# Turning the finished y with DRAM scratch transfers and 32x32 block transposes on VectorE instead of TensorE transposes

## What is computed

```python
h = rms_norm(x, norm_g)
proj = h @ w_in                              # 4096 x ~14000
y_a = sigmoid(ao) * rms_norm(mlstm(...)) * silu(az)      # 1024 columns
y_b = sparse_attention(...) * silu(bz)                   # 2048 columns
y_c = rms_norm(gated_delta(...)) * silu(cz)              # 1024 columns
y = concatenate([y_a, y_b, y_c], axis=-1)    # 256 x 4096
return x + y @ w_out                         # w_out 4096 x 4096
```

## Time and profile before

| what | us |
|---|---|
| median of 3 runs | 1605.11 (1604.88 to 1605.93) |
| the profiled execution, its own time | 1605.32 |
| its span in the trace | 1603.6 |
| PE busy | 1593.8 (99%) |
| DVE busy | 933.5 (58%) |
| ACT busy | 769.3 (48%) |
| POOL busy | 31.3 (2%) |

### The profile page before, as it was taken

How to read it: one execution, slowest core, us unless ns; L and a number is a source line. 1 busy time by engine, 2 the same in 40 slices (tenths; PEclk the granted TensorE clock), 3 DMA queues, 4 the chain that set the end, 5 groups by cost and what they waited for, 6 DMA issues and landing times.

```text
span 1603.6 us, 19082 instructions
## 1 busy us (share of the span) xinstructions
PE 1593.8 (99%) x7456; PEld 1318.2 (82%) x7456; DVE 933.5 (58%) x1410; ACT 769.3 (48%) x1044; POOL 31.3 (2%) x60
## 2 busy tenths in 40 slices
PE   8999999999999999999999999999999999999999
PEld 6888888888888888888778888888888888888887
DVE  5655555557667445574488565564446666665454
ACT  6644444487443334454545455454445434444332
POOL 1000000000011000000000000000001000000000
PEclk9999999999999999999999999999999999999999
DMA  8656666756567554556555555556665655556674
GB/s 290 185 174 206 186 195 184 189 160 185 156 197 210 158 155 145 159 171 192 163 158 178 175 173 163 163 174 206 187 190 187 235 175 171 182 173 195 190 243 158
DMA packets 164006, 294.15 MB, mean 183 GB/s; under 512 B 22458, under 2 KB 27212, under 8 KB 163916
## 3 DMA queue, kind: packets, MB, share of 16 engines
q1 hardware_dynamic: 161084, 284.02, 58.5%
q0 software_dynamic: 2832, 8.92, 1.7%
HBM read 288.17 MB, written 4.72 MB: 183 GB/s over the span
## 4 chain that ended last, share of the span: by engine, by line
PE 98%; DVE 1%; ACT 0%; DMA 0%; issue 0%; SPq 0%
PE acc L584 30%; PE acc L586 30%; PE acc L585 30%; PE mix L557 3%; PE mix L683 2%; PE mix L805 1%; PE mix L665 0%; PE mix L786 0%; DVE w_lo L1248 0%; PE mix L641 0%; PE mix L824 0%; DMA w_raw<-in_w_in_dram 0%; ACT w_hi L917 0%; PE mix L783 0%; PE mix L768 0%
## 5 line engine op out<-in xcount | busy, mean ns | idle before, releaser
L1248 DVE TENSOR_TENSOR w_lo<-w_raw,w_hi 128x1024 fp32r<-128x1024 f32 (+1 forms) x536 | 646.1, 1217 | 468.5 <-ACT w_hi L917 466.2
L584 PE MATMUL acc<-w_hi,op_hi 128*128 128x512 f32 (+1 forms) x2048 | 815.5, 398 | 0.9 <-DVE w_lo L1248 0.9
L586 PE MATMUL acc<-w_hi,op_lo 128*128 128x512 f32 (+1 forms) x2048 | 800.4, 391 | 0.0
L585 PE MATMUL acc<-w_lo,op_hi 128*128 128x512 f32 (+1 forms) x2048 | 798.8, 390 | 0.0
L917 ACT ACTIVATE w_hi<-w_raw 128x1024 fp32r<-128x1024 f32 (+1 forms) x536 | 557.5, 1050 | 461.2 <-PE acc L586 452.6
L586 PEld LDWEIGHTS acc<-w_hi,op_lo 128*128 128x128 f32 x2048 | 385.0, 188 | 82.2
L584 PEld LDWEIGHTS acc<-w_hi,op_hi 128*128 128x128 f32 x2048 | 385.6, 188 | 79.7 <-DVE w_lo L1248 2.7
L585 PEld LDWEIGHTS acc<-w_lo,op_hi 128*128 128x128 f32 x2048 | 385.9, 188 | 75.5
L1380 DVE SCALAR_TENSOR_TENSOR cT<-mix,par,cT 128x255 f32<-128x255 f32 (+2 forms) x72 | 29.1, 474 | 18.2 <-ACT cT L1009 18.2
L1148 ACT ACTIVATE b_p<-b_s,st 128x128 f32<-128x128 f32 (+1 forms) x32 | 14.2, 446 | 49.1 <-DVE st L1585 49.1
L584 PE MATMUL acc<-w_hi,cq_hi 128*128 128x512 f32 x84 | 33.9, 403 | 0.0
(11 more groups left out here) (270 smaller groups left out, 764.2 us busy)
## 6 DMA issues: line engine op xcount, KB each, us to landing
w_raw<-in_w_in_dram SPq DMA_DIRECT2D x368, 512.0 KB, 4.0
w_raw<-in_w_out_dram SPq DMA_DIRECT2D x128, 512.0 KB, 3.8
w_raw<-in_w_in_dram SPq DMA_DIRECT2D x16, 384.0 KB, 3.4
w_raw<-in_a_wuq_dram SPq DMA_DIRECT2D x12, 512.0 KB, 3.8
xs<-in_x_dram SPq DMA_DIRECT2D x7, 512.0 KB, 6.7
w_raw<-in_a_wuqi_dram SPq DMA_DIRECT2D x6, 512.0 KB, 3.5
y<-in_x_dram POOLq DMA_DIRECT2D x6, 512.0 KB, 8.9
out_dram<-y POOLq DMA_DIRECT2D x5, 512.0 KB, 6.1
```

What stands on the lines that cost most here:

```text
L584: nc.tensor.matmul(o, hi[:, kt, tok], hv[:, i, :], start=(kt == blk["kts"][0]), stop=False)
L585: nc.tensor.matmul(o, hi[:, kt, tok], lv[:, i, :], start=False, stop=False)
L586: last_mm = nc.tensor.matmul(o, lo[:, kt, tok], hv[:, i, :], start=False, stop=(kt == blk["kts"][-1]))
L1248: vec.tensor_tensor(split_ap(w_lo, c), w_raw[:, c % RAW_BUFS, 0:n], split_ap(w_hi, c).bitcast(F32), ALU.subtract).then_inc(lo_ready, 1)
```

## The change

PE has no part in "yt" any more, and the piece uses no PSUM bank. In its place:

- POOL moves y through a DRAM scratch, in two parts: r = 1 (columns 1024 to 4095) after "bo" (3, 2) and c_y, r = 0 (columns 0 to 1023) after the last "ay". For each part it issues 8 stores from 32 partitions each, in runs of 32 fp32 numbers (128 B), waits for all 8, and issues 8 loads into 32 partitions each, in runs of 256 numbers (1 KB), back into the same columns of y. A store of r = 1 has 32 x 96 = 3072 runs, a load 32 x 12 = 384; for r = 0 these are 1024 and 128. After this every 32x32 block stands at its place, not yet turned inside.
- A new piece "yd" i on DVE transposes the 32x32 blocks of 128x512 numbers of y in place. "yd" 4 to 15 are in slots 367, 369, ... 389; each waits for all 8 loads of its part.
- "yt" i on ACT and DVE reads y in SBUF instead of the bank. ACT waits for "yd" i and for PE to be done with the slice of op_hi that it overwrites. "yt" 4 to 15 are now in slots 398 to 409; "yd" i and "yt" i for i = 0 to 3 together in slots 481, 483, 485 and 487.
- The reload of x comes behind the stores and loads of r = 1 on POOL; its six loads into y wait for 12 "yt" low parts. The stores and loads of r = 0 come behind the reload.

```diff
@@ plan()
-    weave(first + 4, [("yt", i) for i in range(4, 16)])
+    weave(end("aqk", 0) + 8, [("yd", i) for i in range(4, 16)], 2)
+    weave(first + 6, [("yt", i) for i in range(4, 16)])
...
-    at = weave(at + 1, [("yt", i) for i in range(4)], 2)
+    at = weave(at + 8, [[("yd", i), ("yt", i)] for i in range(4)], 2)
@@ layout
+        y_range = [(0, W_A // P), (W_A // P, KT)]
+        y_dram = [nc.dram_tensor(f"y_dram{r}", (32, z - a, 4, 4 * M, 32), F32) for r, (a, z) in enumerate(y_range)]
+
+        def y_columns(i):
+
+            r = 0 if 2 * i < W_A // P else 1
+            a, z = y_range[r]
+            n = (z - a) // M
+            k = 2 * i - a
+            return y[:, k // n, a * P + SEQ * (k % n):a * P + SEQ * (k % n) + 2 * SEQ]
@@ gpsimd
+            def y_blocks(r):
+
+                a, z = y_range[r]
+                n = (z - a) // M
+                for m in range(M):
+                    for i in range(4):
+                        pool.dma_start(y_dram[r][:, :, :, 4 * m + i, :].rearrange("a k j b -> a (k j) b"),
+                                       y[32 * i:32 * i + 32, m, a * P:z * P].rearrange("p (f b) -> p f b", b=32)
+                                       ).then_inc(y_kept[r], 16)
+                pool.wait_ge(y_kept[r], 16 * 4 * M)
+                for q in range(M):
+                    for j in range(4):
+                        pool.dma_start(y[32 * j:32 * j + 32, q, a * P:z * P].rearrange("p (k t) -> p k t", k=n),
+                                       y_dram[r][:, q * n:q * n + n, j].rearrange("a k i b -> a k (i b)")
+                                       ).then_inc(y_moved[r], 16)
+
             wait_read(pool, "bo", (HKV - 1, 2))
+            pool.wait_ge(c_y, len(UNITS))
+            y_blocks(1)
             for n in range(D // 512):
                 if 512 * n == W_A:
-                    for i in range(12, 16):
-                        wait_read(pool, "yt", i)
+                    pool.wait_ge(y_lo_ready, KT // 2 - 4)
                 pool.dma_start(out_acc(n), x_dram[:, :, 512 * n:512 * n + 512]).then_inc(x_again[n], 16)
+            pool.wait_ge(a_y, H_A)
+            y_blocks(0)
@@ tensor
-                        wait_read(pe, "yt", kt // 2)
+                        pe.wait_ge(y_lo_ready, (kt // 2 + 12) % 16 + 1)
...
-            def yt(i, use):
...
-                for j in range(2):
-                    for m in range(M):
-                        ins = turn(bank(use)[:, j * SEQ + m * P:j * SEQ + m * P + P],
-                                   y[:, m, (2 * i + j) * P:(2 * i + j) * P + P])
-                end_fill(ins, use)
@@ scalar, yt
-                wait_filled(act, use)
+                y_split[0] += 1
+                act.wait_ge(y_turned, y_split[0])
+                b_av = next(b for b, x_ in enumerate(blocks) if x_["kind"] == "av" and x_["arg"] == 1)
+                if i < KT // 2 - 1:
+                    act.wait_ge(split_used, last[b_av] - (KT // 2 - 1) + i + 1 - b_av)
+                else:
+                    act.wait_ge(acc_ready, b_av + 1)
...
-                    ins = func(op_hi[:, kt, :], bank(use)[:, j * SEQ:j * SEQ + SEQ], ACT.Copy,
+                    ins = func(op_hi[:, kt, :], y_columns(i)[:, j * SEQ:j * SEQ + SEQ], ACT.Copy,
@@ vector
+            def yd(i, use):
+                dve.wait_ge(y_moved[0 if i < 4 else 1], 16 * 4 * M)
+                vec.transpose(y_columns(i), y_columns(i)).then_inc(y_turned, 1)
+
             def yt(i, use):
...
-                    src, hi = bank(use)[:, j * SEQ:j * SEQ + SEQ], op_hi[:, kt, :].bitcast(F32)
+                    src, hi = y_columns(i)[:, j * SEQ:j * SEQ + SEQ], op_hi[:, kt, :].bitcast(F32)
...
-                done_bank(ins, use)
+                ins.then_inc(y_lo_ready, 1)
```

More of the change, by code:

```diff
@@ L83 @@
         "ck": 1, "cs": 1, "cr": 1, "co": 2, "bt": 1, "bkt": 2, "bit": 2, "bsc": 2, "bqt": 2, "bs": 1, "bp": 1,
-        "bo": 1, "at": 2, "ae": 2, "ap": 1, "yt": 1}
+        "bo": 1, "at": 2, "ae": 2, "ap": 1}
 def plan():
@@ L352, in hybrid_kernel @@
         y_hi_ready = sem("y_hi_ready")
+        y_kept = [sem(f"y_kept{r}") for r in range(2)]
+        y_moved = [sem(f"y_moved{r}") for r in range(2)]
+        y_turned = sem("y_turned")
+        y_lo_ready = sem("y_lo_ready")
         x_again = [sem(f"x_again{n}") for n in range(D // 512)]
@@ L864, in _ @@
                           cs=cs, cr=cr, co=co, bt=bt, bkt=bkt, bit=bit, bsc=bsc, bqt=bqt, bs=bs, bp=bp, bo=bo,
-                          at=at, ae=ae, ap=ap, yt=yt)
+                          at=at, ae=ae, ap=ap)
             def x_columns(i):
@@ L1174, in ap @@
                 ins.then_inc(a_ss, 1)
+            y_split = [0]
             def yt(i, use):
-                wait_filled(act, use)
+                y_split[0] += 1
[5 more added lines that the diff above has]
+                    act.wait_ge(acc_ready, b_av + 1)
                 for j in range(2):
@@ L1657, in _ @@
                           co=co, cy=cy, bn=bn, bt=bt, bkn=bkn, bqn=bqn, bsc=bsc, btk=btk, bts=bts, bs=bs, bo=bo, at=at, ae=ae, ap=ap, ay=ay,
-                          yt=yt)
+                          yd=yd, yt=yt)
             def x_lo(i):
```

## The result

The changed kernel takes 1621.18 us (median of 4 runs, 1620.88 to 1621.93) against 1605.22 us before (4 runs): ratio 1.010, interval 1.0088 to 1.0113. It is 16.0 us slower; I had forecast 4.6 us slower, in a range that reached to 1630. The profiled execution took 1621.14 us with a span of 1619.4 us.

A forecast was written before the change was run, and what follows sets the result against it. The prediction took PE's own instruction order, busy 99% of the span, as the bound. From 1605.1 us it subtracted 7.75 for the removed turns and added a 12.4 us stall: 1609.8 us, range 1597 to 1630.

The forecast's parts named there:

- the main case: Whole kernel: PE stall from 5.7 us to some 6 us more than 12.4, time 1603 to 1616 us, chance 0.54.
- Gain of the turns: PE: all 16 "yt" pieces leave it, saving 12 x 0.484 + 4 x 0.485 = 7.75 us, all on the path.
- the fourth rival: PE: slower matmuls behind a piece stay, 0.35 us saved per piece instead of 0.485, 1612 us; chance 0.05.
- The stall behind the first "yd": DVE waits in slot 367 from 1116.8 for all upper transfers; PE lacks weights and stalls 12.4 us.
- The stores of r = 1: Upper three quarters of y: 3.15 MB at 60.6 engine-us per MB and 9.6 engines, 19.8 us.
- The loads: Upper three quarters of y: start 1119.3, share engines with weights until 1128.1, then have all; 19.0 us at x's share.
- the rival of half of the paths: Transfers of y on 32 partitions reach half of 377 GB/s; landed 1140.8, stall 17.7 us, 1615.1 us; chance 0.13.
- Landing: Upper loads of y landed at 1135.5, against 1123.1 for no PE stall; 1128.8 with the lower price.
- The clock: PE: a long stall could lower its clock, but the page shows full grant at the start, so nothing added.
- POOL as the bound: Issue of one upper store takes over 2.5 us; at 7.0 us, stall 44 us and 1641 us; chance 0.15.
- The lower quarter: r = 0 transfers: 18.4 us from 1426.9, landed 1445.3, before slot 481 at 1448.7; free, about 11 us to spare.
- "Hidden": Upper transfers land before 1123.1, nothing stalls, and the whole 7.75 us stay: 1597.3 us; chance 0.13.

The follow-up runs named there:

- run 2: Also spelled no_moves: changed kernel without the 32 transfers of y, their semaphores raised at once, y not regrouped; 1597.32 us, ratio 0.995 to before.
- Run 1: Also spelled late_yd: changed kernel with its twelve upper block transposes moved to slots 385 to 396, one per slot; 1601.31 us, ratio 0.9974 to before.
- run 3: Changed kernel with each of the 16 loads of y spread over 128 partitions instead of 32, same bytes and run length, wrong blocks fetched; 1616.51 us.
- stores_long: Also numbered 5: changed kernel with each store writing whole rows of 12 KB (4 KB lower quarter) from its 32 partitions instead of 128 B runs; 1612.38 us.
- run 7: Changed kernel with upper columns moved as three parts, each when finished: 1598.16 us with transposes in slots 385 to 396, 1597.64 us in the changed kernel's slots.
- run 6: Changed kernel with stores and loads issued for partition groups in order 0, 2, 1, 3 instead of 0, 1, 2, 3; 1621.63 us.

## Why the prediction was right in direction and too small in size

The mechanism, one wait of DVE behind the transfers that starves PE, is the one that ran. The size was not: the miss is 11.4 us (1621.2 against 1609.8), 8.8 of it in the gap (21.2 against 12.4), 1.95 in the clock and 0.36 ahead of 84 us, which leaves 0.3. The gap of 21.04 us is over the 20 us which the prediction itself gave as a sign of being wrong. The time lies above the 1603 to 1616 which it gave to the main case, and is inside the full range because that took in a partly slow POOL; this was part of what happened, but in another form than priced.

- **Gain of the turns, 7.75 us:** right, 7.8 us in run 2; the fourth rival is out.
- **DVE's transposes, 0.69 us each, free but for the first:** right, 0.705 us.
- **The stall behind the first "yd":** right in mechanism and place. DVE reached it at 1117.2 (1116.8 forecast), PE ran dry at 1125.7 (1125.1). Run 1, and runs 3 and 5 by their landings, move it as the chain says.
- **The stores of r = 1, 19.8 us of traffic:** this step failed. They took 28.3 us. The price was mis-sized: 73.7 engine-us per MB, where the thin lane traffic gave 60.6, a factor of 1.22 or 4.4 us. The share while the queue had work, 58.8%, was near x's 60.1% (0.4 us), but only because the weights ran out at the end; beside running weights it was 54.0%. And 3.7 us are the hole behind POOL's stop, for which the sum had no term. 19.8 + 4.4 + 0.4 + 3.7 = 28.3.
- **The loads, 14.9 us of traffic:** the size held (1128.8 to some 1143.5), by luck, since two errors cancelled. The price was 75 instead of 58, which is what the rival of half of the paths expects (218 GB/s, where it had 188); but the weights had stopped by the time the loads began, so these had every engine from the start.
- **Landing:** 1144.8 instead of 1135.5; 9.3 us, almost all from the stores. The stall follows, 21.0 instead of 12.4 us; PE ran dry 0.6 us later than forecast.
- **The clock, nothing:** wrong, 1.95 us. And the start of the kernel did not show full speed. The page and the windows print 1.00 there, but the matmuls behind PE's wait start 0.43 us apart, as behind the gap, until 13 us (kernel before, timeline of PE and the window over it):

```profile
9.11 0.63 PE L585 MATMUL acc<-w_lo,op_hi 128*128 128x512 f32 x1
9.54 0.63 PE L586 MATMUL acc<-w_hi,op_lo 128*128 128x512 f32 x1
...
13.25 0.39 PE L586 MATMUL acc<-w_hi,op_lo 128*128 128x512 f32 x1
...
10.00:12.00 2.00, 2.00 (x6) 1.61 (x5) 1.17 (x1) 0.44 (x1) 0.00 (x0) 1.00 1.04 402
```

The record of the clock in that trace begins only at 13.1 us. The spacing of the matmuls was the row to read.

- **POOL as the bound:** no. It is busy 1.3 us per store (10.5 us for the eight), near the 1.2 us of the lane's slope. But it stopped for 13.7 us behind its fifth store, and 3.7 us of that left its queue empty. The rival had the cost in the wrong place, in the time to issue a store.
- **The lower quarter, free:** right. POOL began its stores at 1444.96, its traffic ended at 1467.9, and DVE's first transpose of it at 1468.96 waits for no DMA. The margin was thinner than the 11 us I gave it.
- **"Hidden":** not for 6.3 MB in one piece even when DVE does not wait for it (run 1), but for the same bytes in three pieces (run 7). That the transfers could also starve the weights without any wait of DVE was in none of my cases: I held the weights' 151 GB/s beside x for given, and beside the 32-partition loads they got 81.

The Trainium skill's rule of 2.0 us plus the bytes at 436 GB/s ("DMA: Bandwidth & Descriptors", section "Anatomy of one DMA") gives 9.2 us each way; the trace has 31.7 us for the stores from issue to landing and 17.4 us for the loads. It does not hold here, for eight transfers each way with the weights beside the stores. The Trainium skill's page "SBUF — State Buffer" puts partitions 0 to 63 behind half of the ports (section on the port swizzle) and 436 GB/s behind all; half of that is an estimate of 218 GB/s, and the loads over 32 partitions ran at 218 GB/s with all engines full. The trace agrees in size, with the caution of run 3; run 6 neither shows nor excludes it.

## What to carry to other kernels

Before a wait is put on an engine that also feeds the critical one, count from the trace what the transfers behind it have to move, in how long runs, and what lead the waiting work has; then release each part when it is finished instead of all at the end. A price per byte from a thin row can be too low for a burst (here by a factor of 1.22). A mean share of the engines hides when a queue was empty: cut the stretch where the issuing engine stops, and look at each piece. The victim of a burst (here the weight stream) needs its own sum. And gaps on TensorE of 2.33 us and more cost more than their length here, while a wait of 0.8 us (no_moves) left the clock at 1.00.

## What the runs showed of the hardware that I had not expected

- The clock: behind gaps of 21.04 us and of 2.33 us alike the first nine matmuls ran with a granted clock of about 0.5 (1.2 GHz) and cost 1.95 and 1.7 us. In the late_yd run, where the gap was the short one, the windows show 0.84 in the 2 us in which the matmuls resume, 0.50 in the next two. Behind the 12.11 us of stores_long it was seven matmuls.
- Stores in runs of 128 B cost 73.7 engine-us per MB (the smaller ones of the lower quarter 0.445 x 9.6 x 16 / 1.04 = 66), rows of 12 KB 55; and the long rows left the weight stream 24% of the engines, the short ones 47% while they ran beside it. The run length alone does not set the share: the lower quarter's stores had 44.5% and the upper ones 54.0% with the same runs, the loads in 1 KB runs 69.3% (run 1), the reload of x in 2 KB runs 60.1%.
- Loads into 32 partitions filled all 16 engines at 218 GB/s (75 engine-us per MB), loads into 128 partitions moved 305 GB/s (50).
- POOL stopped behind its fifth store of 3072 runs in all five kernels that have such stores, for 11.9 to 14.1 us, and its queue ran empty for 2.9 to 5.5 us of that. Which limit this is stays open.
- Open as well: what of the loads' 75 is the SBUF side and what the layout of the scratch.
